# First-layer attention of a two-layer trunk: heads in pairs, mask on the matrix engine, compressed branch and part of the output projection moved into it

## The reference

```python
kc = compress(kc_raw, cmp_pos_k, cmp_k_w1, cmp_k_w2)      # 15 blocks of 32 tokens, an MLP with gelu
kc = apply_rope(kc, cos[:, cmp_end], sin[:, cmp_end])
vc = compress(vc_raw, cmp_pos_v, cmp_v_w1, cmp_v_w2)
p_c = masked_softmax(s_c, cmp_end[None, :] <= tq[:, None])   # compressed branch
p_s = masked_softmax(s_s, m_s)                               # selected blocks; top-k takes all 4, so causal
p_w = masked_softmax(s_w, m_w)                               # window of 512 > 256, so causal
out = gb[..., 0:1] * o_c + gb[..., 1:2] * o_s + gb[..., 2:3] * o_w
```

## Time and profile before

| what | value |
|---|---|
| three runs, us | 861.02, 860.29, 860.80 (median 860.8) |
| the profiled execution | 859.9 us, of which the span of the trace is 858.2 us |
| mean granted TensorE clock | 0.958 |
| PE busy | 783.9 us (91%), 6719 instructions |
| DVE, ACT, POOL busy | 497.5, 412.4, 102.0 us |
| share of the chain that ended last | PE 74%, DVE 15%, ACT 6% |
| first attention unit's scores, to the first product of the up projection | 128.65 to 230.58 us |

### The profile page before, as it was taken

The page is one execution under the profiler, slowest core; times in us unless marked ns, Lnnn a source line. Parts: engine busy times, 40 slices in busy tenths (PEclk is TensorE's granted clock), DMA queues, the critical chain, the costliest instruction groups (busy, mean ns, idle before and its releaser), DMA issues.

```text
span 858.2 us, 15701 instructions
## 1 busy us (share of the span) xinstructions
PE 783.9 (91%) x6719; PEld 666.5 (78%) x6719; DVE 497.5 (58%) x847; ACT 412.4 (48%) x640; POOL 102.0 (12%) x153
## 2 busy tenths in 40 slices
PE   4998848999999999999988978999959999999997
PEld 3887736666888888888877965999848888888885
DVE  5665765553576666554469795434534766665432
ACT  6644554443485555633577623442314755555511
POOL 3000205663000000000061003520000000000000
PEclk9999867999999999999999986999969999999999
DMA  9746600000645555556463322000005555555521
GB/s 302 271 129 223 221 0 1 1 1 1 212 157 196 190 175 178 193 196 193 152 209 99 116 93 87 4 4 5 4 1 160 200 167 186 197 196 175 181 86 50
DMA packets 78279, 111.74 MB, mean 130 GB/s; under 512 B 2124, under 2 KB 63714, under 8 KB 78210
## 3 DMA queue, kind: packets, MB, share of 16 engines
q1 hardware_dynamic: 77090, 107.67, 37.7%
q0 software_dynamic: 976, 3.04, 1.2%
q10 hardware_dynamic: 144, 0.04, 0.0%
HBM read 109.68 MB, written 1.05 MB: 129 GB/s over the span
## 4 chain that ended last, share of the span: by engine, by line
PE 74%; DVE 15%; ACT 6%; issue 2%; DMA 1%; POOL 1%; SPq 0%; DVEq 0%; ACTq 0%
PE ps L818 18%; PE ps L986 9%; PE ps L820 9%; PE ps L623 9%; PE ps L625 9%; PE ps L624 9%; PE ps L767 5%; DVE w_lo L1534 4%; PE ps L727 3%; ACT w_hi L1145 2%; PE ps L739 2%; DVE x_hi_lo L1688 1%; DMA w_raw<-w_mem_kv 1%; DMA w_raw<-nsa_cmp_v_w 1%; ACT x_hi_lo L1267 1%
## 5 line engine op out<-in xcount | busy, mean ns | idle before, releaser
L1534 DVE TENSOR_TENSOR w_lo<-w_raw,w_hi 128x2048 fp32r<-128x2048 f32 (+1 forms) x101 | 227.7, 2268 | 118.5 <-ACT w_hi L1145 118.4
L818 PE MATMUL ps<-x_hi_lo,w_hi 128*128 128x512 f32 x640 | 226.5, 399 | 0.0
L1145 ACT ACTIVATE w_hi<-w_raw 128x2048 fp32r<-128x2048 f32 (+1 forms) x101 | 189.1, 1891 | 73.2 <-PE ps L625 64.2
L820 PE MATMUL ps<-x_hi_lo,w_lo 128*128 128x256 f32 x640 | 179.7, 281 | 0.0
L818 PEld LDWEIGHTS ps<-x_hi_lo,w_hi 128*128 128x128 f32 x640 | 120.3, 188 | 29.8
L820 PEld LDWEIGHTS ps<-x_hi_lo,w_lo 128*128 128x128 f32 x640 | 120.9, 189 | 0.0
L623 PE MATMUL ps<-w_hi,x_hi_lo 128*128 128x512 f32 (+2 forms) x240 | 83.3, 347 | 6.7 <-DVE x_hi_lo L1688 3.0
L625 PE MATMUL ps<-w_hi,x_hi_lo 128*128 128x512 f32 (+2 forms) x240 | 82.4, 343 | 0.0
L624 PE MATMUL ps<-w_lo,x_hi_lo 128*128 128x512 f32 (+2 forms) x240 | 82.3, 343 | 0.0
L623 PE MATMUL ps<-w_hi,hidden_hi 128*128 128x512 f32 x176 | 69.6, 395 | 0.0
L625 PE MATMUL ps<-w_hi,hidden_lo 128*128 128x512 f32 x176 | 69.5, 395 | 0.0
(11 more groups left out here) (357 smaller groups left out, 1212.5 us busy)
## 6 DMA issues: line engine op xcount, KB each, us to landing
w_raw<-w_ffn_in SPq DMA_DIRECT2D x44, 1024.0 KB, 5.1
w_raw<-w_ffn_out SPq DMA_DIRECT2D x22, 1024.0 KB, 5.0
w_raw<-rwkv_w_in SPq DMA_DIRECT2D x11, 1024.0 KB, 5.3
w_raw<-nsa_w_in SPq DMA_DIRECT2D x8, 1024.0 KB, 11.2
w_raw<-w_out SPq DMA_DIRECT2D x8, 1024.0 KB, 4.9
w_raw<-w_mem_kv SPq DMA_DIRECT2D x2, 1024.0 KB, 9.2
w_raw<-nsa_cmp_k_w SPq DMA_DIRECT2D x2, 1024.0 KB, 5.6
w_raw<-nsa_cmp_v_w SPq DMA_DIRECT2D x2, 1024.0 KB, 5.6
```

Source lines behind the costliest of these rows:

```text
L818: pe.matmul(psum[:, bank + j, :], kt_of(w_hi, i, k)[:, c], xx[:, k, :, :].rearrange("p c n -> p (c n)"), start=k == 0, stop=False)
L820: ins = pe.matmul(psum[:, bank + j, 0:SEQ], kt_of(w_lo, i, k)[:, c], xh[:, k, :], start=False, stop=k == KD - 1)
L1145: act.activation(w_hi[:, i % SPL, 0:size(i)], raw[:, i % RAW, 0:size(i)], ACT.Copy).then_inc(hi_done, 1)
L1534: dve.tensor_tensor(w_lo[:, i % RAW, 0:size(i)], raw[:, i % RAW, 0:size(i)], w_hi[:, i % SPL, 0:size(i)], ALU.subtract).then_inc(lo_done, 1)
```

## The change

- A unit becomes a pair of heads (f) and one tile. There are 12 units with two branches and 4 memory units in layer 0, and 4 in layer 1. In layer 0 the memory units come first, then tile 0 of the six head pairs, then tile 1.
- Scores: the two heads of the pair use the two halves of the rows and have a bank each; the four score products alternate between them. The mask is added by a product of the rounded identity with the rounded mask into the same bank. DVE then takes the maximum of all branches and both heads straight from PSUM in one instruction, ACT takes the exponentials from PSUM, and there is no masked copy by DVE. Two sets of score banks instead of three.
- Of the four probability blocks POOL scales three and DVE the fourth. Transposes of the first head go to bank 4 (copied by ACT), of the second to bank 5 (copied by DVE); memory units alternate. One set of banks instead of three.
- Values: the two heads alternate, each in its half of the output rows. The high and low parts are written after every unit.
- The compressed branch has its blocks padded to 32 columns: 6 transposes instead of 24, with four heads in one. Its MLP, scores, softmax and transposes stand between the first seven steps of the attention.
- Ahead of the attention, turns, rotations and the splitting of the key input are earlier in the streams: turns 0 to 2 in the middle of projection group 4, turns 3 to 5 in the middle of group 5, turns 6 to 9 before `cmp_gemm(0)`, turn 10 between the two compression products.
- The output projection of tile 0 (all four pieces) is issued in the last four steps of the attention, after the last scores; tile 1 follows. Weight pieces are split at fixed steps (12 and 14) inside the attention, and one in `join` between tile 0's scale and its transposes.
- The zeroing and mask semaphores of layer 1 are merged, with no change to the instructions.

```diff
-        nsa_units = [(f, e, t, "nsa") for f in range(FT) for e in range(2) for t in range(TT)]
-        mem_units = [(f, e, t, "mem") for f in range(FT, KD) for e in range(2) for t in range(TT)]
-        UNITS = [nsa_units + mem_units, mem_units]
+        nsa_units = [(f, t, "nsa") for t in range(TT) for f in range(FT)]
+        mem_units = [(f, t, "mem") for f in range(FT, KD) for t in range(TT)]
+        UNITS = [mem_units + nsa_units, mem_units]
-        SC_BANK, PT_BANK = (0, 1, 4), (2, 3, 5)
-        LAG_T, LAG_V = 3, 5
+        SC_BANK = ((2, 3), (0, 1))
+        LAG_T, LAG_V = 3, 4
...
             def scores(layer, i):
-                if u >= SLOTS:
-                    pe.wait_ge(a_max, u - SLOTS + 1)
+                if u >= 2:
+                    pe.wait_ge(a_exp, u - 1)
                 for b in range(nbr):
+                    for e in range(2):
+                        r = rows_of(e)
...
+                        ins = pe.matmul(psum[:, SC_BANK[u % 2][e], b * SEQ:b * SEQ + nk * P], lhs, rhs, start=b == 0,
+                                        stop=kind == "mem")
+                if kind == "nsa":
+                    for e in range(2):
+                        own = psum[:, SC_BANK[u % 2][e], :].rearrange("p (b n) -> p b n", b=2)[:, :, tile(t)]
+                        ins = pe.matmul(own, ident_r[:], cmask_r[:], start=False, stop=True)
                 ins.then_inc(a_sc, 1)
...
             def attention(layer):
                 n = len(UNITS[layer])
                 for s in range(n + LAG_V):
                     if s < n:
                         scores(layer, s)
+                    if layer == 0 and s == 1:
+                        hidden_turns()
+                    if layer == 0 and s == 2:
+                        block_mlp()
+                    if layer == 0 and s == NMEM + LAG_T:
+                        pe.wait_ge(b_pt, TT)
+                        pe.wait_ge(cmp_set, 2)
                     if 0 <= s - LAG_T < n:
                         probs_turn(layer, s - LAG_T)
+                    if layer == 0 and s == 3:
+                        block_key_turn()
                     if 0 <= s - LAG_V < n:
                         values(layer, s - LAG_V)
+                    if layer == 0 and s == 4:
+                        block_scores()
+                    if layer == 0 and s == 6:
+                        block_turns()
+                    if layer == 0 and s >= n:
+                        out_tile0(0, s - n)
...
+            def exps(layer, i):                      # ACT
+                for e in range(2):
+                    for b in range(nbr):
+                        ins = act.activation(SM[layer][:, u % SLOTS, e, b, 0:nk * P],
+                                             psum[:, SC_BANK[u % 2][e], b * SEQ:b * SEQ + nk * P], ACT.Exp, ...
+            def attention(layer):                    # ACT; DVE's has maxima, factors, probs_out, values_lo
+                    if s < n:
+                        exps(layer, s)
...
+                    if 0 <= s - LAG_T < n:
+                        probs_out(layer, s - LAG_T)
...
+                    if 0 <= s - LAG_V < n:
+                        values_hi(layer, s - LAG_V)
+                    if layer == 0 and s in (12, 14):
+                        split_to(first["out", 0] + (4 if s == 12 else 5))
+            def maxima(layer, i):                    # DVE
+                link(dve.tensor_reduce(mx[:, u % SLOTS, 0:n], src[:, :, 0:nk * P], AX.X, ALU.max))
+                dve.tensor_scalar(nbias[:, u % SLOTS, 0:n], mx[:, u % SLOTS, 0:n], -SCALE, None, ALU.mult).then_inc(a_max, 1)
...
-            full_gemm(first["out", 0], OUT_ORDER, 0, xh, xl)
+            pe.wait_ge(a_lo, N_UNITS - NMEM)
+            full_gemm(first["out", 0], [(j, 1) for j in range(N_OUT)], N_OUT, 0, xh, xl)
```

More of the change, by code:

```diff
@@ L671, in token_gemm @@
                 for hf in range(2):
+                    if hf and between is not None:
+                        between()
                     pe.wait_ge(lo_done, i0 + hf + 1)
@@ new lines, in block_key_turn, with block_scores @@
+            def block_key_turn():
+                n = GROUPS * NCMP
+                pe.wait_ge(c_kd, 2)
+                pe.transpose(psum[:, 5, 256:256 + n], kcd[:].rearrange("p c d -> p (c d)"), ident[0:n, 0:n]).then_inc(c_kt, 1)
+            def block_scores():
+                pe.wait_ge(c_ev, 2)
+                for t in range(TT):
+                    for head in range(HEADS):
+                        r = rows_of(head)
+                        g = head // (HEADS // GROUPS)
+                        c = NCMP * (FT * t + head // 2)
+                        ins = pe.matmul(psum[:, 5 + 2 * (head % 2), c:c + NCMP], qT[r, head // 2, tile(t)],
+                                        kcT[r, g * NCMP:(g + 1) * NCMP], start=True, stop=True)
+                ins.then_inc(b_sc, 1)
@@ L770, in attention, with block_turns @@
+            def block_turns():
+                pe.wait_ge(b_p, TT)
+                for t in range(TT):
+                    for q in range(GROUPS):
+                        ins = pe.transpose(psum[:, 5 + 2 * t, q * P:(q + 1) * P],
+                                           sc[:, t, 4 * q:4 * q + 4, :].rearrange("p h n -> p (h n)"), ident[:])
+                    ins.then_inc(b_tp, 1)
             def attention(layer):
@@ L843, in ffn @@
                 pe.wait_ge(up_mul, w0 + NFC - 2)
-                full_gemm(first["down", layer], DOWN_ORDER, 2 * layer + 1, hh, hl, up_lo, NFC * layer, NFC)
+                full_gemm(first["down", layer], DOWN_ORDER, N_DOWN, 2 * layer + 1, hh, hl, up_lo, NFC * layer, NFC)
             pe.wait_ge(consts, 1)
@@ L884, in _, with block_input_turns, query_turns @@
-            ins.then_inc(c_w2, 1)
-            for k in range(7, NTURN):
-                turn(k)
-            pe.wait_ge(c_kd, 1)
-            pe.transpose(psum[:, 7, 256:256 + n], kcd[:].rearrange("p c d -> p (c d)"), ident[0:n, 0:n]).then_inc(c_kt, 1)
-            pe.wait_ge(c_ktv, 1)
+            def block_input_turns():
+                pe.wait_ge(dup_c, 4)
+                for k in range(3):
+                    turn(k)
+            def query_turns():
+                pe.wait_ge(roped_q, 1)
+                for k in range(3, 6):
+                    turn(k)
@@ L900, in _ @@
[L900 to L907 removed]
+            pe.wait_ge(c_gelu, 2)
             attention(0)
[L909 to L910 removed]
+            pe.wait_ge(a_lo, N_UNITS - NMEM)
@@ L1130, in _ @@
             pe.wait_ge(y_lo, NCH)
-            full_gemm(first["out", 1], OUT_ORDER, 2, xh, xl)
+            full_gemm(first["out", 1], OUT_ORDER, N_OUT, 2, xh, xl)
             ffn(1)
@@ new lines, in attention @@
+                    if layer == 0 and s == 4:
+                        block_scores_out()
+                    if layer == 0 and s == 5:
+                        block_probs()
+                    if 0 <= s - LAG_T < n:
+                        probs_out(layer, s - LAG_T)
+                    if 0 <= s - LAG_V < n:
+                        values_lo(layer, s - LAG_V)
+                    if layer == 0 and s in (12, 14):
+                        split_to(first["out", 0] + (4 if s == 12 else 5))
@@ L1793, in _ @@
-            i = first["cmp"]
-            split_to(i + 3 + AHEAD)
+                if g == 2:
+                    dve.wait_ge(tok_evA, 3)
+                    dve.wait_ge(tok_evD, 3)
+                    rope_heads(0, HEADS, [rtq[:, k] for k in range(4)], roped_q)
+                if g == 3:
+                    dve.wait_ge(tok_evA, 4)
+                    dve.wait_ge(tok_evD, 4)
+                    rope_heads(O_KS, GROUPS, small, roped_k)
+                if g == 4:
+                    dve.wait_ge(tok_evA, 5)
+                    dve.wait_ge(tok_evD, 5)
+                    dve.wait_ge(roped_k, 1)
+                    rope_heads(O_KW, GROUPS, small, roped_k)
@@ L1843, in _ @@
             attention(0)
-            split_to(first["out", 0] + N_OUT + 2)
+            split_to(first["out", 0] + N_OUT + 1)
             join(0, first["out", 0] + N_OUT)
```

612 lines of the change are left out of this document (341 added, 271 removed).

## The result

| | before | after |
|---|---|---|
| median of the runs, us | 860.5 (856.3 to 861.0) | 832.5 (828.2 to 833.7) |
| ratio | | 0.967, interval 0.9615 to 0.9717 |
| profiled execution, us (its span) | 859.9 (858.2) | 832.0 (830.3) |

The change wins 28 us. The forecast was 14 (847.0, range 832 to 865): the sign and the places were right, the size was half.

A forecast was written before the change was run, and what follows sets the result against it. TensorE was taken as the bound from 145 to 190 us, with about 17 us of waits before; afterwards ring and TensorE nearly even. 10.0 won up to the up product plus 4 in layer 1 gave 847 us, range 832 to 865.

The forecast's parts named there:

- The start of the attention: First score product at 104.5 us, against 128.65 before, with key turns moved earlier.
- The ring: Each step's dependent maximum, exponentials, copy, high part, low part, before the next maximum: 4.55 us in tile 1, 3.3 in tile 0.
- steps 0 to 6: Memory units, two tile-0 units and compressed branch: 30 us, including 8 for the branch and 3 for the clock; mark 134.5.
- steps 7 to 9: Tile-0 steps: three at 3.3 us, plus 3 for a clock that rises late; mark 147.4.
- steps 10 to 14: Five steps at 4.7 us, plus 7.4 for the splits at 12 and 14 and 4 for the clock; mark 182.3.
- tail: Last softmax, transposes, values 8.4 us, tile 0's projection 11, then tile 1's 11.4; first up product at 220.6.
- The clock terms "+3", "+3" and "+4": Microseconds added for low clock in steps 0 to 6, steps 7 to 9, and behind the splits at 12 and 14.
- The step of 4.7 and 3.3: Microseconds per attention step, tile 1 and tile 0, with ring and TensorE nearly even; two heads cost 6.1 and 3.9 before.
- the middle, 2.1 and 1.4: TensorE's value products per pair, us: tile 1 between bounds 1.38 and 2.76, tile 0 between 0.94 and 1.88.
- Rival 1: The clock never falls and column halves overlap fully: 834 us; chance 0.18.
- Rivals 2 and 3: Values do not overlap: 853 us, chance 0.14; pairing does nothing on TensorE, scores too: 861, chance 0.07.
- Rival 4: TensorE stays at half clock through the pairs, steps costing twice its work: 37 more, 884 us; chance 0.09.

The follow-up runs named there:

- splits_late: Kernel after with the two weight splits of steps 12 and 14 moved to steps 16 and 17, behind tile 0's products; 824.5 us, ratio 0.953.
- tail_off: Kernel after with tile 0's output projection issued behind the attention instead of in its last steps; 835.2 us, ratio 0.966.
- both_serial_b: Kernel after with scores and values of a pair's two heads issued one head after the other; 836.7 us, ratio 0.974.
- values_serial: Kernel after with the value products of the two heads issued one head after the other instead of alternating; 833.9 us, ratio 0.966.
- fill: Kernel after with thirty products without use issued in front of TensorE's two long waits at the splits; 831.5 us, ratio 0.968.
- ring_late: splits_late with VectorE's low part one step later, behind the next maximum; 824.7 us, ratio 0.959.
- all_three: ring_late with the compressed branch's scores issued at step 5 instead of 4 and its softmax at step 6; 826.1 us, ratio 0.963.
- ring_warm: ring_late with the ten score and mask products of step 6 issued twice; 823.0 us, ratio 0.959.
- ring_from8: splits_late with VectorE's low part one step later only from step 8 on; 818.0 us, ratio 0.954.

## Why the prediction was half right

**What held.** The start of the attention: 104.5 forecast, 103.0 measured. The ring as the bound of the steps, and the splits in it, 3.7 us each forecast and 3.80 measured (7.87 - 4.07). Layer 1, 4 won against 4.07 (it takes 15.6 to 16.9 us in the other runs). splits_late confirms the price of the splits, and tail_off that tile 0's projection is TensorE's own time wherever it stands (0.9 us apart).

The tail, 38.3 against 38.7, is luck in part: the four sets of values took 6.7 us in place of 8.4, and the projection with its norm 24.2 in place of 22.4, of which 1.2 is low clock.

**What failed.** The 12.3 us by which the up product came earlier than 220.6, by step:

| step | forecast | after | |
|---|---|---|---|
| start | 104.5 | 103.0 | -1.5 |
| steps 0 to 6 | 30.0 | 28.4 | -1.6 |
| steps 7 to 9 | 12.9 | 9.3 | -3.6 |
| steps 10 to 14 | 34.9 | 29.0 | -5.9 |
| tail | 38.3 | 38.7 | +0.4 |

1. *The clock terms "+3", "+3" and "+4".* This is the step that failed: the forecast paid for every fall of the clock as if TensorE ended each step behind it. Of the seven us of the last two terms about 1.8 came, 0.6 of it up to maximum 15. In steps 7 to 9 there was no half clock: 131 to 136 is at 0.89 and 136 to 141 at 1.00, so the second "+3" (taken from 134 to 145 in the earlier trace rows) was nothing. That stretch of before isn't what follows every gap: a fall of the clock costs only where TensorE ends the step. Step 5 shows it best: ended by the branch's softmax, it takes 6.50 us in the kernel after, 4.3 of them at low clock, and 6.49 and 6.50 in tail_off and both_serial_b, all of it at 0.50. Step 4 is ended by TensorE's 48 small products (4.18 us, 5.31 in tail_off at 0.50, 2.85 before at 1.00), and it takes 9.52, 11.56 in tail_off and 7.51 in values_serial, where these products had 1.00 and took 2.85: there the first "+3" had a place, of some 1.3 us (4.18 - 2.85). They came from the "+4": 0.6 in step 14 and 1.2 in the tail, which went with the splits (splits_late); fill took back 1.8. But it was no empty term: ring_late and all_three had that half clock through steps 7 to 9 and 7 to 11; ring_late lost 3.6 to 3.9 us by it up to maximum 15, going by ring_warm.
2. *The step of 4.7 and 3.3.* Measured 4.07 and 3.11: 5 x 0.63 + 3 x 0.19 = 3.7 us. Two sizes were off. TensorE's part, "the middle, 2.1 and 1.4" for the values, was the bound "1.38" and "0.94" itself: 16 instructions in 1.02 and four of the compressed branch in 0.36 are 1.38 for two heads, to the hundredth what one head cost; tile 0 has 0.59 + 0.36 = 0.95 against 0.94. A step of tile 1 is then 1.07 + 0.35 + 1.0 + 1.38 = 3.8, under the ring. (The sum also put tile 1's values into every step from 10 on. With the lag of four, steps 10 and 11 still carry tile 0's, and TensorE's part there is 1.07 + 0.35 + 0.55 + 0.95 = 2.9.) And the ring, "4.55", is 4.07: its copy of ACT's share was 0.28 and not 0.57 (it is a tile-0 pair's; tile 1's takes 0.49, from step 13 on), the exponentials 1.56 and not 1.8, high and low part with the hand-over 0.47 and not 0.55, the maximum 1.14 and not 1.23.
3. *The start and steps 0 to 6*, 3.1 us together, are inside their bounds. The wait for the block scores is what makes step 4 long (VectorE: maxima 4 and 5 at 111.40 and 120.92, and 5.37 us of waiting for the 48 small products between them):

```profile
111.40 0.69 DVE L1747 TENSOR_REDUCE row_max<-ps 128x4 f32<-128x512 f32 x1 [0.43 <-PE ps L776]
...
117.96 0.41 DVE L1811 TENSOR_TENSOR block_scores<-ps,block_mask 128x90 f32<-128x90 f32 x2 [5.37 <-PE ps L862]
...
120.92 0.68 DVE L1747 TENSOR_REDUCE row_max<-ps 128x4 f32<-128x512 f32 x1
```

The section "The mechanism" of the Trainium skill's page "TensorE: Matmul & The Clock Gate" was weighed in the forecast: a weight load overlaps only where its row group differs. For the value products, which share their rows and differ in columns, this trace disagrees. Sixteen instructions of two heads take the 1.02 us that eight of one head took before (158.18 to 159.20 there), 64 ns apiece against 127, and 94 in eights:

```profile
158.18 1.09 PE L767 MATMUL ps<-probsT,nsa_proj 128*64 128x128 f32 x8
159.20 0.43 PE L767 MATMUL ps<-block_probsT,vc_tok 15*64 15x128 f32 x2
```

The two heads' instructions start 6 to 7 ns apart, and a pair follows the pair before by 109 ns. The middle that I took between the bounds was too much by 0.7 us of TensorE's time a set.

**The rivals.** Rival 1 (the clock never falls, column halves overlap fully, 834) came nearest, 832.5 measured: the second half was exact, the first was true of steps 7 to 12 alone, and the clock did fall in steps 4 to 6, in step 14 and in the tail. That its sum came within 2 us is luck in part: it took 0.5 us off the steps where 3.7 came, and not all of the clock's 10 us came back. I gave it 0.18, with the two stalls as the reason against it; but these stalls were already in my sum with only 4 of the 10 us. Rivals 2 and 3 fall with the 1.02 us of a pair's value products and the 1.07 of its scores. Rival 4 didn't come in this kernel; ring_late, with one VectorE instruction moved besides the splits, shows a piece of it.

**What stays open.** Whether unpaired heads would be slower in the new pipeline, since no run took the pairs apart; what the earlier turns, the padding and the mask on TensorE are worth each, since no run took one of them back; why the attention's clock recovered in after at about 132 us and in all_three only at 156; the 1.6 us of the last feed-forward; and how much of ring_from8's median is the edit.

## What to carry to other kernels

Before adding a price for a low clock, find out which engine ends that step: half a clock cost nothing in step 5, which softmax ends, and 2 us in step 4, which TensorE ends. One late instruction of another engine may turn the first case into the second, as steps 7 and 8 of ring_late suggest. Write the cross-engine ring of each loop down (here maximum, exponentials, copy, high part, low part), and keep everything that isn't needed in it outside: two weight splits placed in it cost 8 us. Where two heads use different halves of the array and their instructions alternate in runs of at most four, count a pair as one, as here.

## What the runs showed of the hardware

- Products on different column halves (128x64 each) overlap wholly: 16 instructions in 1.02 us against 8 in 1.02 before. With eight of the same half in a row it is 1.51, with four in a row there is no loss (tile 0's eight in 0.59 in both orders). Score products on row halves lose nothing either (1.07 for eight instructions in both orders, 1.06 for four in before).
- The clock stayed at 0.50 from 112.6 to 146.7 us in ring_late, through 13.66 us of work in 15.4, a wait of 2.61 us, and 9.16 us of work in the 10 from 131 to 141. With that wait filled (ring_warm) it was back at 1.00 at 134.4.
- Thirty products without use, issued where the kernel after waits 4.57 us, kept the clock at 1.00 (162 to 166) where it had been 0.50. Placed ahead of the second wait, they didn't.
- A product of 128x512 went at 0.233 us in the last feed-forward of the kernel before and at 0.227 in every run of the changed one, at a granted clock of 1.00 in both.
